# Extra gate slots at the ends of attention rounds, shared additions in the merge, and a gather between expert loads

## The reference

```python
h = rms_norm(x, norm1_g[l]);  z = h @ w_in[l]
oa = mixer_a(...)   # 8 heads, dense attention, rotary positions
ob = mixer_b(...)   # 8 heads, low-rank q and kv, dense attention
oc = mixer_c(...)   # 8 heads, window of 128, distance bias, sink column
ox = memory_cross_attention(...)   # 4 heads on 256 memory rows
gates = sigmoid(z[..., IN_G:])     # 4 x 1024 columns
merged = sum over the branches b of gates[b] * (o_b @ w_branch[b])
x = x + merged @ w_out[l]
x = x + expert_choice_moe(rms_norm(x, norm2_g[l]), ...)  # 16 experts, 32 + 64 rows each
```

## Time and profile before

| | |
|---|---|
| median of three runs | 3306.27 us (3300.39 to 3307.9) |
| profiled execution | 3304.8 us, its span 3303.0 us |
| mean granted TensorE clock | 0.975 |
| TensorE busy | 3068.3 us (93%) |
| VectorE (DVE), ScalarE (ACT), GpSimd (POOL) busy | 2140.1 (65%), 1955.4 (59%), 449.0 us (14%) |
| chain that ended last | PE 79%, DVE 9%, ACT 5%, issue 2%, POOL 1%, DMA 1% |

### The profile page before, as it was taken

One profiled execution on the slowest core, in us unless ns is written; L12 is line 12 of the kernel. 1 busy time (PEld: TensorE's weight loads), 2 busy tenths in 40 slices (PEclk: granted clock), 3 DMA queues, 4 the chain that ended last, 5 costly groups with the idle time before them and its releaser, 6 DMA issues.

```text
span 3303.0 us, 47435 instructions
## 1 busy us (share of the span) xinstructions
PE 3068.3 (93%) x17028; PEld 2471.2 (75%) x17028; DVE 2140.1 (65%) x3000; ACT 1955.4 (59%) x3094; POOL 449.0 (14%) x524
## 2 busy tenths in 40 slices
PE   7999999899989799999999999998999969999997
PEld 7977877677877577777699787777778756777775
DVE  4565544664464788888846654556654548888886
ACT  4366455555443677777744655555554337777775
POOL 0021001111150111111000211111112301111110
PEclk9999999999999899999999999999999989999999
DMA  6112111123632999999941121112226249999996
GB/s 228 54 58 71 47 47 41 53 77 104 231 119 91 345 389 380 388 388 381 353 141 51 55 70 47 51 42 73 71 100 253 99 167 348 383 390 380 389 388 245
DMA packets 265538, 626.51 MB, mean 190 GB/s; under 512 B 15008, under 2 KB 86688, under 8 KB 265280
## 3 DMA queue, kind: packets, MB, share of 16 engines
q1 hardware_dynamic: 257904, 595.18, 48.6%
q0 software_dynamic: 7472, 29.17, 3.5%
HBM read 564.54 MB, written 66.06 MB: 191 GB/s over the span
## 4 chain that ended last, share of the span: by engine, by line
PE 79%; DVE 9%; ACT 5%; issue 2%; POOL 1%; DMA 1%; DVEq 1%; ACTq 0%; POOLq 0%; SPq 0%
PE bank L1983 17%; PE bank L1985 17%; PE bank L1984 17%; PE bank L2043 12%; PE bank L2075 3%; PE bank L2067 2%; PE bank L2094 2%; PE bank L2095 2%; PE bank L2182 1%; PE bank L2298 1%; PE bank L2184 1%; POOL PR L886 1%; ACT PH L1143 1%; DVE PL L1683 1%; PE bank L2064 1%
## 5 line engine op out<-in xcount | busy, mean ns | idle before, releaser
L1431 DVE TENSOR_TENSOR mlo<-mraw,wlo 128x2048 fp32r<-128x2048 f32 x160 | 366.2, 2289 | 112.6 <-ACT wlo L976 109.6
L1984 PE MATMUL bank<-mlo,xsT_hi 128*96 128x512 f32 x1024 | 402.7, 393 | 0.0
L886 POOL TENSOR_SCALAR PR<-PR,prec 128x256 f32<-128x256 f32 (+2 forms) x336 | 191.2, 570 | 1444.7 <-DVE prec L1707 1444.7
L2043 PE MATMUL bank<-hT_lo,whi 128*128 128x512 f32 (+1 forms) x1024 | 383.0, 374 | 0.0
L2043 PE MATMUL bank<-hT_hi,whi 128*128 128x512 f32 (+1 forms) x1024 | 359.1, 351 | 11.7 <-ACT fgs L970 11.7
L976 ACT ACTIVATE wlo<-mraw 128x2048 fp32r<-128x2048 f32 x160 | 305.6, 1911 | 87.2 <-DMA mraw<-in_w_gate_up_dram 62.7
L2043 PE MATMUL bank<-hT_hi,wlo 128*128 128x512 f32 (+1 forms) x1024 | 351.5, 343 | 0.0
L1431 DVE TENSOR_TENSOR mlo<-mraw,whi 128x2048 fp32r<-128x2048 f32 x128 | 290.2, 2288 | 26.9 <-ACT whi L976 26.7
L1143 ACT ACTIVATE PH<-bank 128x256 fp32r<-128x256 f32 (+2 forms) x336 | 159.0, 473 | 219.0 <-PE bank L2095 125.6
L1666 DVE TENSOR_REDUCE nmax<-bank 128x1 f32<-128x512 f32 (+1 forms) x240 | 134.6, 562 | 236.6 <-PE bank L2067 178.3
L1983 PE MATMUL bank<-whi,hT_hi 128*128 128x256 f32 (+1 forms) x960 | 272.8, 284 | 0.0
(11 more groups left out here) (313 smaller groups left out, 7737.6 us busy)
## 6 DMA issues: line engine op xcount, KB each, us to landing
mraw<-in_w_gate_up_dram SPq DMA_DIRECT2D x128, 2048.0 KB, 12.2
mraw_d<-in_w_down_dram SPq DMA_DIRECT2D x96, 1024.0 KB, 16.2
wraw<-in_w_in_dram SPq DMA_DIRECT2D x50, 1024.0 KB, 5.9
mraw<-in_w_down_dram SPq DMA_DIRECT2D x32, 1024.0 KB, 16.8
G<-g_cols SPq DMA_DIRECT2D x16, 1536.0 KB, 10.1
g_cols<-fgs SPq DMA_DIRECT2D x64, 256.0 KB, 2.0
mw_raw<-in_w_branch_dram SPq DMA_DIRECT2D x14, 1024.0 KB, 5.1
o_raw<-o_rows SPq DMA_DIRECT2D x6, 1536.0 KB, 8.6
```

What stands on the lines that cost most here:

```text
L886: pool.tensor_scalar(PR[:, u % 3, 0:n], PR[:, u % 3, 0:n], prec[:, u % 4:u % 4 + 1], 1.0, ALU.mult, ALU.mult).then_inc(p_norm.sem, 1)
L1431: dve.tensor_tensor(m_lo(pos), m_raw(pos), m_hi(pos), ALU.subtract)\
L1984: pe.matmul(out, lhs_hi, rhs_lo, start=False, stop=False)
L2043: ins = pe.matmul(gate_banks[i % 2][:, 0:n], lhs, rhs, start=m == 0, stop=m == 3 * KD - 1)
```

## The change

`gate_slots` deals a gate into more slots: one more at unit 0 of a round's first chunk (two in C), and one behind the last unit of its last chunk, ahead of the last products with the values. ACT's copies follow. `v_high` moves behind the first two exponentials, DVE's part for it behind unit 0. The roots move to between rounds, with a load of the exponential's table after them; the squares of B's inputs move to A's first round, the memory keys' norm is cut in four, B's sums of squares come one unit later, and the low parts of A and C are dealt among the first maxima. In the merge, DVE adds the odd columns of X's two steps itself, C's outputs are cut at step 2, the output weights and X's outputs earlier, and the order of ACT's and DVE's last parts changes. SP loads three of the four pairs ahead of the last tile's stores and the fourth after the gather; the first gather reads its index without a copy, and DVE waits until it is issued.

```diff
-def gate_slots(per, front, chunk):
+def gate_slots(name, chunk, chunks):
+    per, front = PER[name], FRONT[name] if chunk == 0 else 0
+    first, behind = FIRST[name] if chunk == 0 else 0, int(chunk == chunks - 1)
+    plan, done = gate_plan(per + front + first + behind)
+    def unit(i):
+        return i - front if i < front else max(0, i - front - first)
...
+FIRST = {"A": 1, "B": 1, "C": 2, "X": 1}
...
 # SP, into the experts
                 for i, t in enumerate(TILES):
+                    if i == NT - 1:
+                        sp.wait_ge(out_mm.sem, out_mm.at(l, 11))
+                        for n in range(3):
+                            load_pair_m(l * NE, n)
                     sp.wait_ge(r2_normed.sem, r2_normed.at(l, i))
...
-                sp.wait_ge(out_mm.sem, out_mm.at(l, 11))
-                for i in range(PAIRS):
-                    load_pair_m(l * NE, i)
                 sp.wait_ge(xs_in.sem, xs_in.at(l, 0))
+                load_pair_m(l * NE, 3)
...
 # POOL
-                for i in range(24):
+                for i in [*range(16), 16, 18, 20, 22]:
...
-                gather(0, 0)
+                pool.indirect_dma_start(XS[:], None, h_rows[:, :], bass.IndirectOffsetOnAxis(ap=idxT[:, 0:1], axis=0))\
+                    .then_inc(xs_in.sem, 16)
+                pool.sem_inc(first_sent.sem, 1)
...
 # ACT, attend
-                v_high(l, br, it)
...
                 exps(1)
+                v_high(l, br, it)
+                for g, i in copies.get(-1, []):
+                    gate_copy(l, g, i)
...
-                    if br.name == "A" and it == 1 and 2 <= u < 2 + NT:
-                        bc_squares(u - 2)
-                    if br.name == "A" and it == 1 and u == 2 + NT:
-                        bc_roots()
+                    if br.name == "A" and it == 0 and 8 <= u < 8 + 2 * NT and u % 2 == 0:
+                        bc_squares((u - 8) // 2)
...
-                    if br.name == "C" and it == 0 and u == 4:
-                        cx_roots(l, 3).then_inc(x_root.sem, 1)
...
                 for it in range(BR["A"].its):
+                    if it == 1:
+                        bc_roots()
+                    act.preload_act_table(ACT.Exp)
                     turned_ac(l, BR["A"], it)
...
                                 roots(l, [(stat[:, 0:24], BQK)], it + PREP_BP)
+                                act.preload_act_table(ACT.Exp)
...
+                cx_roots(l, 3).then_inc(x_root.sem, 1)
+                act.preload_act_table(ACT.Exp)
                 for it in range(BR["C"].its):
...
 # ACT, merge
-                    if p in (0, 3):
+                    if p in (0, 2):
                         for k in range(4):
-                            o_high(l, (p + 1) // 2 + (p == 0), k)
+                            o_high(l, (1, None, 2)[p], k)
...
-                for c in range(2, 4):
-                    merged_high(c)
-                for q in (2, 3):
-                    out_high(q)
-                    for c in range(2 * q, 2 * q + 2):
-                        merged_high(c)
+                out_high(2)
+                merged_high(2)
+                merged_high(3)
+                out_high(3)
+                for c in range(4, KD):
+                    merged_high(c)
...
 # DVE, attend
+                for i in range(4 if br.name in "AC" else 0):
+                    low_ac(l, br, it, i)
                 for u in range(ahead):
+                    if br.name in "AC":
+                        low_ac(l, br, it, 4 + u)
...
-                    if br.name == "A" and it == 0 and u == 4:
-                        norm_mem(l)
+                    if br.name == "A" and it == 0 and u in (13, 15, 17, 19):
+                        norm_mem(l, (u - 13) // 2)
...
-                if u in CX_AT and (it, CX_AT[u]) in CX_PIECES:
+                if u - 1 in CX_AT and (it, CX_AT[u - 1]) in CX_PIECES:
...
 # DVE, merge and into the experts
+                        if own:
+                            dve.wait_ge(br_ev.sem, br_ev.at(l, 8 * p + 2 * i + 1))
+                            dve.tensor_tensor(mT[:, c, :], mT[:, c, :], gp[:, 1, :], ALU.add).then_inc(acc_own.sem, 1)
...
+                        if p >= 6 and c >= 2:
+                            merged_low(c - 2)
+                for c in range(6, KD):
                     merged_low(c)
                 for q in (2, 3):
                     out_low(q)
...
+                dve.wait_ge(first_sent.sem, first_sent.at(l, 0))
                 lo_moe(l, 0, 0)
...
 # PE
-                        pe.wait_ge(prep_lo.sem, prep_lo.at(l, m0 + 5))
+                        pe.wait_ge(prep_lo.sem, prep_lo.at(l, m0 + min(5, 3 + u)))
...
+                for i, m in gate_slots(br.name, nu // per - 1, nu // per)[0][per]:
+                    gate_part(l, g0 + nu // per - 1, i, m, j0 + nu // per - 1)
                 for v in due:
                     output(v)
```

More of the change, by code:

```diff
@@ L150, in gate_plan @@
     return plan, done
-def gate_slots(per, front, chunk):
[L155 to L158, removed]
+def gate_slots(name, chunk, chunks):
[4 more added lines that the diff above has]
+        return i - front if i < front else max(0, i - front - first)
+    units = {}
+    for i, parts in enumerate(plan):
+        units.setdefault(unit(i), []).extend(parts)
+    done = {i: max(-1, unit(n)) for i, n in done.items()}
+    for u, parts in units.items():
+        assert all(i < 2 or m or u > done[i - 2] + (done[i - 2] >= 0) for i, m in parts)
+    return units, done
 PER = {"A": 12, "B": 12, "C": 8, "X": 12}
 FRONT = {"A": 5, "B": 0, "C": 5, "X": 0}
+FIRST = {"A": 1, "B": 1, "C": 2, "X": 1}
 HI_AT = {12: (1, 3, 5, 7), 8: (0, 2, 3, 5)}
@@ L529, in build @@
         br_ev = sig("br_ev", 64)
-        acc_made = sig("acc_made", 24)
+        acc_made = sig("acc_made", 20)
+        acc_own = sig("acc_own", 4)
         mt_hi = sig("mt_hi", KD)
@@ L1110, in attend @@
                 for c in range(nu // per):
-                    _, done = gate_slots(per, FRONT[br.name], c)
+                    _, done = gate_slots(br.name, c, nu // per)
                     for i in range(4):
-                        copies.setdefault(c * per + done[i] + 1, []).append((g0 + c, i))
+                        copies.setdefault(c * per + done[i] + (done[i] >= 0), []).append((g0 + c, i))
                 def exps(u):
@@ L1160, in attend @@
                         hi_quarter(l, HI_AT[per].index(u % per), *halves[u // per])
-                for g, i in copies.get(nu, []):
-                    gate_copy(l, g, i)
+                for u in (nu, nu + 1):
+                    for g, i in copies.get(u, []):
+                        gate_copy(l, g, i)
                 for u in (nu - 2, nu - 1):
@@ L1530, in norms_a, with norm_mem @@
                 dve.drain()
-            def norm_mem(l):
-                by_stat(mkv[:, :, 0:256], 0, MT, 4, HD, stat_m)
-                dve.drain()
-                by_gain(mkv[:, :, 0:256], g_head[:, 5, :], MT, 4, HD)
+            def norm_mem(l, n):
+                t = slice(n % 2 * 2, n % 2 * 2 + 2)
+                if n < 2:
+                    by_stat(mkv[:, t, 0:256], n * 8, 2, 4, HD, stat_m)
+                else:
+                    dve.drain()
+                    by_gain(mkv[:, t, 0:256], g_head[:, 5, :], 2, 4, HD)
             def cx_norm(l, it, u):
-                if u in CX_AT and (it, CX_AT[u]) in CX_PIECES:
-                    h = CX_AT[u]
+                if u - 1 in CX_AT and (it, CX_AT[u - 1]) in CX_PIECES:
+                    h = CX_AT[u - 1]
                     n = CX_PIECES.index((it, h))
@@ L1832, in _ @@
                         dve.wait_ge(g_sig.sem, g_sig.at(l, 4 * p + i))
-                        n0 = 4 * (p - 2) + i
+                        n0, c = 4 * (p - 2) + i, 4 * (p % 2) + i
+                        own = p >= 6 and c % 2 == 1
                         for h, (t0, n) in enumerate(((256, 512), (0, 256))):
@@ L1856, in _ @@
                     out_low(q)
-                    for c in range(2 * q, 2 * q + 2):
-                        merged_low(c)
                 def residual(g):
@@ L2050, in attend @@
                 per, g0 = PER[br.name], gate_of(br.name, it)
-                front = FRONT[br.name]
-                if not front:
+                if not FRONT[br.name]:
                     pe.wait_ge(prep_ev.sem, prep_ev.at(l, it * br.nprep + (br.prep0 + br.nprep - 1)))
@@ L2103, in attend @@
                         scores(u + 2)
-                    for i, m in gate_slots(per, front, u // per)[0][u % per + (front if u < per else 0)]:
+                    for i, m in gate_slots(br.name, u // per, nu // per)[0][u % per]:
                         gate_part(l, g0 + u // per, i, m, j0 + u // per)
@@ L2127, in heads_ac @@
                         if i:
-                            for part, m in gate_slots(per, front, 0)[0][i - 1]:
+                            for part, m in gate_slots(br.name, 0, len(br.units) // per)[0][i - 1 - front]:
```

85 lines of the change are left out of this document (45 added, 40 removed).

## The result

The changed kernel takes **3226.51 us** (median of 4 runs, 3225.86 to 3228.17) where the kernel before takes 3303.33 in the runs beside it (3299.86 to 3307.9): a ratio of 0.9765, 95% interval 0.9752 to 0.9777. The forecast was 3216, its range 3190 to 3256: the sign and the range hold, the point was 10 us too low. In the traces the span falls from 3303.0 to 3224.7, by 78.3 us where the sum had 90.

A forecast was written before the change was run, and what follows sets the result against it. TensorE, the busiest engine, bounds the kernel, so its waits in the attention rounds, merge and way into the experts can be won. Terms sum to 90 us off 3304.8, 3215, or 3216 us to the median; range 3190 to 3256.

The forecast's parts named there:

- Ends: Ends of attention rounds: a gate slot behind the last unit covers TensorE's wait, 22.5 falling to 3.5 us, -19.
- The cover is merely moved: Rival, chance 0.20: what the ends of rounds gain opens again inside the units; 3254 us.
- B's squares: B's units 3 and 6: sums one unit later find ACT's square ready, -22; fourth round +1.
- A's extras: A's early rounds: memory keys' norm in four pieces, -3.7; B's input squares and roots moved out of round 1, -8.
- Starts: Starts of rounds: earlier scores and an extra gate slot outweigh the roots delaying K's copy, together -7.5.
- C's roots and gate copies: C: roots leave unit 4 of its first round, -3.5; one of three gate-bank waits a round goes, -4.
- Thinner cover: Attention units: slots put at the ends are taken from the units, giving back +2.5.
- Clock: Attention: of 12 half-clock stretches 8 go and two or so come, -10, bounds 0 and -20.
- Merge: Merge: C's low parts at step 2 end a wait, -3; shared additions at the tail 0, bounds -4 and +6.
- Gather: Way into the experts: rows land 4.5 us after issue; -6.4 a layer, -13 in all, bounds -18 and +5.
- late stores: Rival, chance 0.06: loads run past 16.5 us, so the gather waits for stores, not the index; 3234 us.

The follow-up runs named there:

- run 1: Changed kernel without the gate slot behind the last unit, its share given back to the units: 3245.8 us.
- run 3: Changed kernel with the six pairs of squares of A's first round taken two at a time at units 8, 12 and 20, where ACT stands idle: 3220.4 us.
- run 11: Changed kernel without the gate slots in front of the first turn of a round, their share given back to the units: 3219.7 us.
- run 6: Changed kernel with SP loading the last gates ahead of the last two output weights, and ACT making columns 2 and 3's high parts before both output weights: 3214.5 us.
- run 9: Changed kernel with DVE held until the gathered rows have landed, not only until the gather is issued: 3228.7 us.
- run 10: Changed kernel with DVE held until a copy that POOL makes behind the gather has run: 3224.3 us.
- run 7: Kernel of run 6 with all 24 merge additions on POOL and DVE's low output weights dealt between its last two low parts: 3221.4 us.
- run 8: Changed kernel with the first expert's four loads behind the last stores, as before the change: 3233.9 us.
- run 2: Changed kernel with B's sums of squares back at units 3 and 6, where the square is made: 3255.0 us.
- run 4: Changed kernel with the roots of A's second and C's first round, and their table loads, at the last unit of the round before: 3220.0 us.
- run 12: Changed kernel with the edits of run 3, run 4, run 6, run 10 and run 11 together: 3197.1 us.

## Why the prediction was right, and where it was off

Its signs came: the wait of the last products with the values is 3.6, no wait for POOL is longer than 1.2 us, the table loads stand between rounds, and the attention has 2 stretches at half clock. Only the gathered rows come 4 us sooner and not 6. Term by term:

- *Ends, -19*: right. 22.5 fell to 3.6, and undoing it costs 19.3. "The cover is merely moved" holds for 2 us of it (run 1).
- *B's squares, -22*: right, rather more; undoing it costs 28.5, waits 24.6 of it.
- *A's extras, -3.7 and -8*: the first right. Of the second, "leave ... for alternate units of round 0" was costed at nothing, and no work was named that hides it: the collision with the outputs' copies costs 2.5 a layer, and undoing it won 6.1 in all (run 3).
- *Starts, -7.5*: the size is right (the waits ahead of scores and first turns fall from 12.9 to 9.3 in the first layer), the reason half wrong. K's wait was put at 1.8 at each of four starts and is 7.0 in all, as foreseen. But "one more gate slot stands ahead of the first turn" is not what helps: run 11 is 6.8 us faster without it.
- *C's roots and gate copies, -3.5 and -4*: about right, 4.4 and 2.9; the third wait for a gate bank in a round falls from 0.98 to 0.26 us, and comes back to 0.97 without the end slots (run 1).
- *Thinner cover, +2.5*: mis-sized. In C alone the small waits behind the first turn, up to the seventh unit after it, rise from 1.2 (its second round before) to 2.5, 5.2 in four rounds. The text blames the end slots, but these waits stay at 2.5 without them (run 1) and are 1.2 to 1.6 without the slots in front (run 11).
- *Clock, -10*: mis-sized the other way: 12 stretches became 2, some 17 us at the 1.7 that were reckoned for each and 12 to 15 at the 1.2 to 1.5 that stages show, which paid for the last two. There is luck in this count, as other traces of the same attention have 0 to 4.
- *Merge*: "issue" fell by 2.9 (forecast 3). The tail lost 2.5 where 0 was taken, inside its bounds. The times that the step worked out are right: it put the second product group 0.5 us sooner than in the old order, and it begins 0.9 and 0.6 sooner behind the first; the waits of both tails fall from 14.5 to 13.5. What it had only in its bound is the clock, behind the second group. It also took the order on ACT that it named, the output weight ahead of column 2, as given; turned round, that and the order of SP's loads are worth some 10 us (run 6).
- *Gather, -13*: 8.2. Of 6.4 a layer, 0.7 were lost because the gather is issued later than was reckoned, and 1.5 to 1.9 because the rows take 6.0 to 6.4 to land. The 4.5 us of an undisturbed gather was right (4.2 to 4.3 in runs 9 and 10). What failed is the sentence before it, that DVE is held back until POOL has issued: held until the issue, DVE runs beside the instruction and makes it three times as long. The order of the stores was a near thing: they were put at 1081 (the terms given add up to 1080.2), just before the index; in the changed kernel the three loads take 18.2 us in the first layer and not 16.5, and the stores land 0.4 us ahead of the index in the first layer and 0.8 in the second, so "late stores" was missed narrowly.

The gains that were named came where they were named. Two of the misses are of one kind, work moved beside work of another engine or ahead of it and costed at nothing: the squares (6.1) and the gather (4.8). The cover was mis-sized by 2.7, and the tail lost 2.5 to the clock. They add up to some 16 us, and the clock in the attention gave 2 to 7 back.

## What to carry to other kernels

Cover is a fixed stock: a slot of TensorE's spare work pays where a wait is certain and as long as the slot (ends of rounds), and costs where the wait was made by an order on another engine, which is better turned round. Before work is moved to a place that looks free, look at that engine's line there for its own idle time (here 2 us ahead of certain turns, and at the end of each round) and put it there, not at every other unit. A hold that is meant to keep an engine quiet during an instruction must hang on something that runs behind that instruction. And before a few microseconds are put down to an edit, look where in the two traces they lie: here up to 5 of them were stretches at half clock at places that the edit does not touch.

## What the runs showed of the hardware

- DVE's subtraction of two SBUF tensors beside it (L1458, 128x2048) slows POOL's indirect DMA instruction from 1.00 to 2.98 us, and the rows land 2 us later (6.2 in the changed kernel, 4.2 to 4.3 in runs 9 and 10). The Trainium skill (GPSIMD Engine Reference, Specifications) says that POOL shares its SBUF interfaces with VectorE and meets contention from instructions with two SBUF inputs; the runs agree, and show that issuing a gather is hit as well. Whether an instruction with one such input does it too was not run.
- Likewise with additions on POOL and subtractions on DVE (run 7): 1.85 becomes 2.4 us on POOL, 0.95 becomes 2.16 and 1.21 becomes 2.84 on DVE.
- A gather of 96 rows lands in 4.2 to 4.3 us with the loads done and DVE held (runs 9 and 10), in 6.2 with the loads done and DVE beside it, and in 9.6 with DVE and four loads of 2 MB beside it (run 8).
- Waits of much the same sum go with very different times at half clock. In the nine traces with the changed kernel's order of the tail (the changed kernel, runs 1 to 4 and 8 to 11), a tail has 6.4 to 8.0 us of waits, the longest of 1.8 to 2.7 us, and 6.8 to 17.1 us at a granted clock of 0.5. In the two with the order turned (runs 6 and 12), a tail has two waits of 1.2 and 3.6 us and 3.4 or 6.8 us at 0.5. What one trace shows of this is not to be taken for the rule.
